# A decode loop with paged caches: page loads counted by halves, and one reduction taken ahead of one copy

## The reference

```
past_nsa = cache_nsa[page_table]          # k_cmp, v_cmp, k_sel, v_sel; 16 pages of 256 KB per sequence
kc, vc   = compress(k_cmp, w_ck), compress(v_cmp, w_cv)
p_c      = softmax(q kc + bias); o_cmp = p_c vc
imp      = p_c m_ov;  keep the best 16 blocks of 64 tokens
o_sel    = softmax(q k_sel over the kept blocks) v_sel
o_win    = softmax(q k_win) v_win         # last 512 tokens
past_mla = cache_mla[page_table]          # latent c_kv and rotated key; 16 pages of 96 KB per sequence
o_lat    = softmax(q_lat c_kv + q_rope k_rope) c_kv
x       += gate * ([o_a * silu(z_a) | (o_lat w_uv) * silu(z_b)] @ w_out), then a final norm
```

## Time and profile before

| | |
|---|---|
| median of 3 executions | 1175.72 us (1175.21 to 1178.54) |
| the profiled execution | 1174.56 us |
| its span, first to last instruction | 1172.8 us |
| PE busy | 1062.1 us, 91% |
| PEld, DVE, ACT, POOL busy | 63%, 51%, 31%, 7% |
| decode rounds 1 to 6 | about 34 us each, 24 us of them PE busy |

### The profile page before, as it was taken

One profiled execution on the slowest core, in us unless ns is written; L12 is line 12 of the kernel. 1 busy time (PEld: TensorE's weight loads), 2 busy tenths in 40 slices (PEclk: granted clock), 3 DMA queues, 4 the chain that ended last, 5 costly groups with the idle time before them and its releaser, 6 DMA issues. The chain is left out here.

```text
span 1172.8 us, 22226 instructions
## 1 busy us (share of the span) xinstructions
PE 1062.1 (91%) x8172; PEld 739.4 (63%) x8172; DVE 600.1 (51%) x1588; ACT 368.3 (31%) x958; POOL 87.9 (7%) x186
## 2 busy tenths in 40 slices
PE   6899999999999999989999999999995786667697
PEld 3455799988876677767766676645543454444466
DVE  0643313543224777696767576333335655545562
ACT  0321001111123655465545555211112223232231
POOL 0210001100000111010000000100002000000000
PEclk8999999999999999999999999999998988888897
DMA  9842430020032500000000000348617776788760
GB/s 353 278 143 81 114 129 3 21 80 1 1 67 50 151 2 1 1 2 1 2 1 2 1 2 1 86 107 238 208 54 195 205 221 199 209 225 243 191 196 20
DMA packets 68755, 119.71 MB, mean 102 GB/s; under 512 B 30337, under 2 KB 47764, under 8 KB 65576
## 3 DMA queue, kind: packets, MB, share of 16 engines
q1 hardware_dynamic: 68648, 118.29, 35.1%
HBM read 103.88 MB, written 14.36 MB: 101 GB/s over the span
## 5 line engine op out<-in xcount | busy, mean ns | idle before, releaser
L549 PE MATMUL PS<-AR 128*128 128x256 f32 (+2 forms) x896 | 219.7, 403 | 0.0
L549 PEld LDWEIGHTS PS<-AR 128*128 128x128 f32 x896 | 167.8, 190 | 45.2 <-issue 6.2
L2089 PE MATMUL PS<-AR 128*128 128x512 f32 x256 | 112.2, 592 | 0.0
L1747 PE MATMUL PS<-CA,AR 128*128 128x128 f32 x704 | 111.4, 282 | 0.8 <-ACT AR L1821 0.8
L1747 PEld LDWEIGHTS PS<-CA,AR 128*128 128x128 f32 x704 | 76.9, 142 | 44.6 <-issue 31.4
L963 DVE TENSOR_TENSOR AR<-PS,AR 128x256 f32<-128x256 f32 (+2 forms) x80 | 36.2, 452 | 132.9 <-PE PS L549 132.7
L1821 ACT ACTIVATE AR<-PS 128x512 f32<-128x512 f32 (+1 forms) x108 | 58.1, 546 | 125.6 <-PE PS L1747 124.9
L1725 PE MATMUL PS<-AR 128*128 128x65 f32 (+1 forms) x688 | 89.3, 271 | 0.0
L1725 PEld LDWEIGHTS PS<-AR 128*128 128x128 f32 x688 | 84.3, 192 | 0.0
L2089 PEld LDWEIGHTS PS<-AR 128*128 128x128 f32 x256 | 47.6, 190 | 54.5 <-issue 54.5
L1806 ACT ACTIVATE AR<-PS,SM_ 128x512 f32<-128x512 f32 (+4 forms) x192 | 76.4, 470 | 15.4 <-DVE SM_ L1914 8.7
(11 more groups left out here) (367 smaller groups left out, 1562.3 us busy)
## 6 DMA issues: line engine op xcount, KB each, us to landing
AR<-in_cache_nsa SPq DMA_DIRECT2D x128, 256.0 KB, 6.4
AR<-in_cache_mla SPq DMA_DIRECT2D x128, 96.0 KB, 5.1
AR<-in_x_prompt SPq DMA_DIRECT2D x16, 512.0 KB, 4.6
AR<-in_w_ada SPq DMA_DIRECT2D x3, 2048.0 KB, 11.5
AR<-in_w_in SPq DMA_DIRECT2D x6, 1024.0 KB, 8.6
AR<-in_w_ada SPq DMA_DIRECT2D x8, 512.0 KB, 4.1
AR<-in_w_out SPq DMA_DIRECT2D x4, 1024.0 KB, 10.2
AR<-in_w_out SPq DMA_DIRECT2D x2, 2048.0 KB, 17.6
```

What stands on the lines that cost most here:

```text
L549: mm = pe.matmul(bank[:, 0:WIDE[g]], tokens[:, k, :], w, start=(fresh and k == 0), stop=(last and k == 3), skip_group_check=True)
L1747: mm = pe.transpose(PS[:, 4 + c % 2, P * (t - t0):P * (t - t0) + P], tile(u, t), ident)
L2089: mm = pe.matmul(PS[0:n, 2 + 2 * (m % 2) + c, :], YTO[m % 2][:, f, 0:n], weights[:, f, 512 * c:512 * c + 512], start=(f == 0), stop=(f == 7))
```

## The change

- The semaphores `s_nsa` are kept by tile (half of the pages) and no longer by the parity of b: `s_nsa[0]` counts the 8 page loads of chunks 0 and 1, `s_nsa[1]` those of chunks 2 and 3, over all b.
- K0 waits for the first eight pages only; K2 gets a wait of its own, for the other eight.
- `selected_turn` on DVE waits for both.
- On DVE the minimum of the latent scores and its spreading operand stand ahead of the wait for "pts" and of its copy, no longer behind them.

```
@@ chunk
-            if name == "K0":
-                pe.wait_ge(s_nsa[b % 2], 256 * (b // 2) + 256)
+            if name in ("K0", "K2"):
+                pe.wait_ge(s_nsa[c // 2], 128 * b + 128)
@@ load_pages
-                    .then_inc(s_nsa[b % 2], 16)
+                    .then_inc(s_nsa[tile], 16)
@@ selected_turn
-                dve.wait_ge(s_nsa[b % 2], 256 * (b // 2) + 256)
+                for tile in range(2):
+                    dve.wait_ge(s_nsa[tile], 128 * b + 128)
@@ dve_decode
-                bank = wait_item(dve, b, "pts")
-                dve.tensor_copy(PTI, bank[:, 0:128]).then_inc(s_rD, 1)
-
                 dve.wait_ge(s_sc, 3 * b + 2)
                 step(dve.tensor_reduce(MN[:, 0:1], PSF[:, S0:S0 + 544], AX, ALU.min))
                 spread(b, 0, 2, MN[:, 0:1])
+
+                bank = wait_item(dve, b, "pts")
+                dve.tensor_copy(PTI, bank[:, 0:128]).then_inc(s_rD, 1)
+
                 bank = wait_item(dve, b, "fmw")
```

## The result

The changed kernel takes 1158.14 us in the median of 4 runs (1154.54 to 1161.06), the kernel before beside it 1175.97 us (4 runs): ratio 0.9843, 95% interval 0.9811 to 0.9875, some 18 us faster. Run once more in a later comparison it took 1155.94 us (6 runs) against 1176.89, ratio 0.9824 (0.9796 to 0.9851). The forecast was 1150.4 us with a range of 1146.5 to 1156: the direction and most of the size were right, and the time lies 2 us above the range (the second median, 1155.94, just inside it). The profiled execution took 1157.52 us, span 1155.7.

What follows compares the result with a forecast made beforehand. Bounds: the ring from page loads through PE, then SP's list. Taking 24.1 us in rounds 0 to 6 plus 1.2 us in round 7 from 1174.56 gave 1149.3; with 1.16 for the median, 1150.4 us, range 1146.5 to 1156.

Steps and rivals of the forecast that it cites:

- What bounds the kernel: Rounds wait on a ring from freed buffer through page loads and K0; behind it SP's own list, 30.2 to 31.3 us.
- Landing of the halves: Page loads: first half in 11.1 us after the first issue, second half taken as 20.5 us.
- From K2 to the end of the round, 6.0 us: From K2 to the next page loads: 6.7 us before, 6.0 after, with ACT's copies no longer behind an exponential.
- SP's rounds: SP's list sets rounds 1 to 5; starts at 952.4, 983.7, then three rounds of 30.2 us to 1074.3.
- Behind K2 is queued everything that ends the round: K2 sets the end of a round, so PE could close it 20.5 + 6.0 = 26.5 us after the page loads.
- The half clock, 0.9 us: PE may run slow behind K2: bounds nothing or 1.7 us lost, 0.9 taken, making 27.4 us per round.
- Edit 2, 1.2 us once: DVE's minimum ahead of the copy of "pts" saves a net 1.2 us, counted only in round 7; bounds 0 and 1.5.
- K2's own start: K2 starts at +21.3 us after the page loads or, with edit 2, just at the second half's landing.
- That the transfers bind: Rival: transfers, 25.4 us of all engines per round, become the bound; 0.02 slower and 0.02 no change, shared with the clock.
- That SP were no bound (1134.6 us): Rival: SP does not limit, so six rounds take 27.4 us each and the kernel 1134.6 us; chance 0.06.
- that the halves signal nothing sooner: Rival: K0 waits for pages as before, only round 7's 1.2 us remain, 1174.5 us; 0.04 with kindred failures.
- a loss by the clock: Rival: PE stays at half clock, about 1238 us; 0.02 slower and 0.02 no change, shared with the transfers.

Runs made afterwards that it cites:

- Experiments 3 to 5: Changed kernel without the page numbers' bounds check, 1144.94 us; page numbers read and checked twice in the changed kernel, 1188.46 us, and in the kernel before, 1192.93 us.
- experiment 6: Changed kernel with DVE's turn of the next window rows moved behind the minimum over fs and the copy of the latent sums: 1150.82 us, ratio 0.9779.
- Experiments 6 and 7: Changed kernel with DVE's window turn moved later, 1150.82 us; changed kernel with window rows and keyed weights issued between the page halves for b >= 2, 1155.05 us.
- e7: Changed kernel with DVE's window turn behind the minimum over fs and page numbers read without bounds check: 1130.70 us, ratio 0.9599.

## Why the prediction was off, step by step

- **What bounds the kernel: right.** The ring through the pages and, hidden behind it, SP's own list. Experiments 3 to 5 show the second, which PE's waits do not name and SP's own do, by the wait that vanishes (17.3 to 1.4 us).
- **Landing of the halves: right.** Where K0 and K2 waited for their pages, in rounds 1 and 6, K0 started 11.3 to 11.6 us after the first load (11.1 forecast) and K2 20.3 to 21.0 (20.5). The waits that were forecast for each round, "a little at K0 and again at K2", did not come in rounds 2 to 5: there DVE's wait for the keyed weights held the end of the round back.
- **From K2 to the end of the round, 6.0 us: right** once nothing else binds (5.9 in experiment 6).
- **SP's rounds: 2.5 us too short.** The sixth start came at 1076.84, not 1074.3: 0.4 us before the first of them, 0.7 us in round 1 (PE ended it 1.3 us behind SP, whose own list was some 0.6 us shorter than forecast), and 1.4 us in the four rounds after, where single issues were slow (12.38 us for one set of pages, 2.16 for one store).
- **"Behind K2 is queued everything that ends the round": the step that failed.** Window rows and keyed weights, issued after the pages, are waited for by DVE's turn (L2880), ahead of the exponential. Before, that turn came at 980.85, 13.7 us after the window rows' issue at 967.13, and rows and weights had landed 3.6 us earlier; the prediction pulled everything up to K2 forward by 6 us and didn't ask what else in that stretch waits for a transfer. In round 6 of the changed kernel DVE reached the turn 17.2 us after the first page load, not 25.7, and the keyed weights landed at 23.15, not at K2's 20.5: 2.65 us more. The path behind the turn is also 0.8 us longer than the 6.0 behind K2 (6.8 at full clock). Experiments 6 and 7 show the step: without the turn in the way the round takes 26.6 us.
- **The half clock, 0.9 us: too small there.** The wait made a gap of 3.49 us on PE right ahead of "ss", key products and window scores, and these took 9.6 us behind the landing against 6.8 at full clock: 2.8 us, 1.9 more than the term. Together (2.65 + 0.8 + 1.9) round 6 took 32.78 instead of 27.4 us, 5.4 of the 8.2 us by which the profiled execution (1157.52) missed 1149.3; SP's 2.5 us are most of the rest.
- **Edit 2, 1.2 us once: not refuted, and hardly measured.** From W_out's load to the end it was 46.08 us against 47.02, 0.9 us less, and "fmw" followed "pts" directly. But this stretch took 41.6 to 46.2 us in the eleven profiles with edit 2, 44.64 in the changed kernel's second one, and 46.7 to 47.2 in the three without it: edit 2 may be worth more than 1.2 us there, and the spread of its clock (0.80 to 0.93) is larger than the term.
- **K2's own start, a slip in the working.** The prediction's 973.7 for latent values already holds edit 2 (979.99 less 6.3), so "+21.3" is K2 with both edits, 0.8 us behind the landing and not "just at" it. Nothing came of it: in round 6 PE stood ready for K2 18.3 us after the first load, and 20.0 us after it in experiment 6.
- **Rivals.** That the transfers bind is not borne out: DMA share times length is 25 to 26 us in rounds 2 to 6, as before, and 28.9 in round 1, while the rounds take 30 us and more. That SP were no bound (1134.6 us) is refuted by experiments 3 to 5; that the halves signal nothing sooner, by the 8.5 us of K0 and K2; a loss by the clock did come, measured at 2 to 3 us in the round that PE ends, and not as a slower kernel. The range was too narrow because it bounded the clock at 1.7 us and left out a landing that no wait of the kernel before had shown.

Open: the spread of the changed kernel (1154.5 to 1161.1 us) has at least three parts, which times do not separate: the prompt (the loop's first page load at 886.2 and 891.8 us in its two profiles), the clock, and the landing of the keyed weights (21.1 to 23.4 us in four profiles). Why the landing and some single issues vary stays open too.

## What to carry to other kernels

When a wait goes, list every transfer that is issued behind the one you freed, and ask of each who waits for it and by how much it was early; a load that was 3.6 us early is late once what waits for it comes some 8 us sooner. An issuing engine's own list, register steps and bounds checks included, is a ring of its own that the waits of the computing engines do not show: add it up from one round's first issue to the next, and look how long the issuing engine itself still waits. Then undo the bounds one at a time: here a reordered DVE step and 16 checks left out, both small, gave 27 us more on top of 18.

## What the runs showed of the hardware

- Reading 16 page numbers cost SP 5.2 to 6.3 us: a register load of 1.2 to 2.3 us, and then some 0.25 us for each checked number. Without the check only the load is left.
- The granted clock fell to half in some rounds and not in others of the same kernel, with PE's gap the same: in e7 PE waited 2.9 to 3.1 us for DVE in each round, and four of six rounds show a clock of 1.00, two 0.94; these two are 1.0 to 1.7 us longer. The Trainium skill ("TensorE: Matmul & The Clock Gate", section "HAM oscillation — how this bites in real kernels") tells of a loop that is throttled again at each wait; for waits of 3 us the trace shows it in some rounds only.
- The sixteen pages landed in their order of issue in each of four rounds looked at, three of the changed kernel and one of the kernel before: in the changed kernel's round 6 the first 3.5 us, the eighth 6.3 us and the last 9.5 us after its issue. The Trainium skill ("DMA: Bandwidth & Descriptors", section "Queues, rings and completion order") says that completion is not first-in first-out for an issuing engine; these rounds show no case of it.
- A 512 KB and a 256 KB load issued right behind sixteen page loads landed 9.1 to 11.6 us after their issue in rounds 1 to 6 of the changed kernel's two profiles; the same load differed by 2 us from round to round.
